# The value projection of an HGRN2 trunk in chunks of 512 features, token blocks apart, scaled out by ScalarE

## The reference

```python
def hgrn2_mixer(xn, w_in, lb, out_gain, w_out):
    proj = xn @ w_in                     # (256, 2048) @ (2048, 8192), float32
    q, fr, v, g = split(proj, 4)
    q = silu(q) * 128 ** -0.5
    f = lb + (1.0 - lb) * sigmoid(fr)
    k = 1.0 - f
    o = chunked_gated_recurrence(q, k, v, log(f))
    return (rms_norm(o, out_gain) * silu(g)) @ w_out
```

## Time and profile before

| | us |
|---|---|
| median of 3 runs (2339.4 to 2339.58) | 2339.45 |
| the profiled execution | 2340.2 |
| its span | 2338.4 |
| TensorE busy (share of the span) | 2328.3 (100%) |
| VectorE busy | 1691.0 (72%) |
| ScalarE busy | 1044.3 (45%) |
| granted TensorE clock | 0.999 |

### The profile page before, as it was taken

How to read it: one execution, slowest core, us unless ns; L and a number is a source line. 1 busy time by engine, 2 the same in 40 slices (tenths; PEclk the granted TensorE clock), 3 DMA queues, 4 the chain that set the end, 5 groups by cost and what they waited for, 6 DMA issues and landing times.

```text
span 2338.4 us, 37346 instructions
## 1 busy us (share of the span) xinstructions
PE 2328.3 (100%) x13212; PEld 2049.6 (88%) x13212; DVE 1691.0 (72%) x2147; ACT 1044.3 (45%) x1146; POOL 2.7 (0%) x8
## 2 busy tenths in 40 slices
PE   9999999999999999999999999999999999999998
PEld 8988888888888888888888888888888888888887
DVE  7978788768788788764545666666788788785444
ACT  7344443554444444434444444444444444443443
POOL 0000000000000000000000000000000000000000
PEclk9999999999999999999999999999999999999999
DMA  7555554565656656656565666565656656665664
GB/s 248 159 171 163 164 177 157 175 197 182 192 179 195 188 181 196 191 187 193 185 194 185 190 188 190 185 194 172 201 184 188 197 180 189 193 205 186 192 191 157
DMA packets 410284, 434.93 MB, mean 186 GB/s; under 512 B 13264, under 2 KB 386384, under 8 KB 410064
## 3 DMA queue, kind: packets, MB, share of 16 engines
q1 hardware_dynamic: 409616, 431.53, 59.1%
q10 hardware_dynamic: 576, 2.16, 0.3%
HBM read 431.54 MB, written 2.10 MB: 185 GB/s over the span
## 4 chain that ended last, share of the span: by engine, by line
PE 98%; DMA 1%; DVE 0%; ACT 0%; SPq 0%; issue 0%; DVEq 0%; ACTq 0%
PE acc L1071 54%; PE acc L1081 28%; PE acc L1117 3%; PE acc L1118 3%; PE acc L1116 3%; PE acc L1094 3%; PE acc L1103 1%; PE side L1233 1%; PE side L1212 0%; DMA h<-in_x 0%; DMA raw<-in_hgrn_w_in 0%; PE side L1228 0%; PE side L1063 0%; DVE w_parts L552 0%; PE side L1051 0%; ACT w_parts L333 0%
## 5 line engine op out<-in xcount | busy, mean ns | idle before, releaser
L552 DVE TENSOR_TENSOR w_parts<-raw,w_parts 128x1024 fp32r<-128x1024 f32 x816 | 979.9, 1222 | 578.9 <-PE acc L1081 417.6
L333 ACT ACTIVATE w_parts<-raw 128x1024 fp32r<-128x1024 f32 x816 | 856.4, 1058 | 990.8 <-PE acc L1071 764.0
L1071 PE MATMUL acc<-xn,w_parts 128*128 128x512 f32 x4352 | 1040.1, 391 | 1.4 <-ACT w_parts L333 1.0
L1071 PEld LDWEIGHTS acc<-xn,w_parts 128*128 128x128 f32 x4352 | 799.5, 188 | 156.4 <-issue 1.2
L1081 PEld LDWEIGHTS acc<-xn,w_parts 128*128 128x128 f32 x4352 | 557.5, 191 | 20.4
L1081 PE MATMUL acc<-xn,w_parts 128*128 128x256 f32 x4352 | 566.8, 283 | 0.0
L1071 PE MATMUL acc<-act,w_parts 128*128 128x512 f32 x1216 | 290.6, 391 | 0.0
L1071 PEld LDWEIGHTS acc<-act,w_parts 128*128 128x128 f32 x1216 | 223.5, 188 | 43.3
L1081 PEld LDWEIGHTS acc<-act,w_parts 128*128 128x128 f32 x1216 | 156.0, 191 | 6.0
L1081 PE MATMUL acc<-act,w_parts 128*128 128x256 f32 x1216 | 157.9, 283 | 0.0
L1116 PE MATMUL acc<-w_parts,act 128*128 128x512 f32 x352 | 137.3, 390 | 0.0
(11 more groups left out here) (124 smaller groups left out, 1020.7 us busy)
## 6 DMA issues: line engine op xcount, KB each, us to landing
raw<-in_ffn_w_up SPq DMA_DIRECT2D x352, 512.0 KB, 3.7
raw<-in_ffn_w_down SPq DMA_DIRECT2D x176, 512.0 KB, 4.3
raw<-in_hgrn_w_in SPq DMA_DIRECT2D x128, 512.0 KB, 3.8
raw<-in_sc_w_in SPq DMA_DIRECT2D x96, 512.0 KB, 4.6
raw<-in_hgrn_w_out SPq DMA_DIRECT2D x32, 512.0 KB, 3.9
raw<-in_sc_w_out SPq DMA_DIRECT2D x32, 512.0 KB, 4.2
h<-in_x SPq DMA_DIRECT2D x4, 512.0 KB, 7.8
final_w<-in_final_norm ACTq DMA_DIRECT2D x1, 1024.0 KB, 7.2
```

Of the source, the lines that this page charges most:

```text
L333: nc.scalar.activation(w_parts[:, c % RING, :, 0, :], raw[:, c % RING], ACT.Copy).then_inc(hi_ready, 1)
L552: v.tensor_tensor(w_parts[:, c % RING, :, 1, :], raw[:, c % RING], w_parts[:, c % RING, :, 0, :].bitcast(F32), ALU.subtract).then_inc(lo_r ...
L1071: o = mm(to[:, j, :], w[:, q, 0, j * P:(j + 1) * P], src[:, k * KW + q, :, :].rearrange("p n t -> p (n t)"), start=begin and q == 0, stop= ...
```

## The change

The value group alone is made in another way. Its chunks become 2 tiles of input features by 512 output features, 8 of them for the whole group, with no halves. A chunk has six matmuls of 512 columns a token block: four with the high part of the weights (tokens high and low, 2 tiles) and two with the low part. All six of a block add up in one bank, bank 0 of set 0 for block 0 and of set 1 for block 1. For a pair of chunks TensorE makes block 0 of both (highs, then lows), then block 1 of the first chunk (highs, lows, side work), then of the second. The wait for low parts is in block 0's lows; `hi_used` and `lo_used` count in block 1. Block 0's last matmul of the group counts `first_values_done`.

At the group's last chunk, behind the split of the chunk four ahead, ScalarE scales block 0 out of its bank into `vt`, then block 1, 512 columns each, and each gives a set back. VectorE has no part in it, `corr` isn't used, and the corrections of the phase are counted without the group's two.

```diff
-HGRN_IN = Phase(None, 4, 4, DT, scales=3)
+V_GROUP = 2
+HGRN_IN = Phase(None, 4, 4, DT, scales=3, wide_group=V_GROUP)
...
+            def values(i, c):
+
+                for b in range(T // P):
+                    if b == 0:
+                        act_e.wait_ge(first_values_done, at(i, 1, 1))
+                    else:
+                        act_e.wait_ge(lo_used, at(i, HGRN_IN.cpi, c + 1 + RING))
+                    nc.scalar.activation(vt[:, :, b, :], acc[:, b, 0, :].rearrange("p (j d) -> p j d", j=TG), ACT.Copy,
+                                         scale=rs[:, T + b:T + b + 1]).then_inc(acc_free, 1)
...
                             if not last:
                                 split(i, phase, c + RING)
-                            if ends and phase.corrections:
+                            if ends and g == phase.wide_group:
+                                values(i, c)
+                            elif ends and phase.corrections:
                                 correction(i, phase, g, part, c)
...
-                if phase is HGRN_IN and g == V_GROUP:
-                    for b in range(T // P):
-                        o = v.scalar_tensor_tensor(
-                            out=vt[:, part * TW:(part + 1) * TW, b, :],
...
+            def value_highs(c, b, src, k, begin):
...
+                for q in range(KC):
+                    for n in range(2):
+                        o = mm(acc[:, b, 0, :], x_block(src, k * KC + q, n, b), w[:, 2 * q:2 * q + 2, 0, :],
+                               start=begin and q == 0 and n == 0, stop=False)
+                return o
...
+            def value_run(i, first, src, chunks, between):
+
+                for b in range(T // P):
+                    for c, k, begin, end in chunks:
+                        if begin:
+                            pe.wait_ge(acc_free, at(i, HGRN_IN.api, V_GROUP * HGRN_IN.parts + b + 1))
+                        if b == 0:
+                            pe.wait_ge(hi_ready, at(i, HGRN_IN.cpi, c + 1))
+                        elif first:
+                            pe.wait_ge(mirror_ready, k * KC // TG + 1)
+                        high = value_highs(c, b, src, k, begin)
+                        if b:
+                            high.then_inc(hi_used, 1)
+                            value_lows(c, b, src, k, end).then_inc(lo_used, 1)
+                            between(c)
+                    if b == 0:
+                        for c, k, begin, end in chunks:
+                            pe.wait_ge(lo_ready, at(i, HGRN_IN.cpi, c + 1 + RING))
+                            low = value_lows(c, b, src, k, end)
+                            if end:
+                                low.then_inc(first_values_done, 1)
```

More of the change, by code:

```diff
@@ L58, with __init__ @@
 class Phase:
-    def __init__(self, before, n, groups, k_tiles, scales=0, corrects=True, parts=2):
+    def __init__(self, before, n, groups, k_tiles, scales=0, corrects=True, parts=2, wide_group=None):
         self.n, self.groups, self.cpg, self.parts = n, groups, k_tiles // KC, parts
         self.cpi, self.api = groups * self.cpg, groups * parts
-        self.scales, self.corrections = scales, self.api if corrects else 0
+        self.wide_group = wide_group
+        wide_parts = 0 if wide_group is None else parts
+        self.scales, self.corrections = scales, self.api - wide_parts if corrects else 0
         self.c0 = before.c0 + before.n * before.cpi if before else 0
@@ L69, in __init__, with wide @@
         assert self.cpi % RING == 0 and self.c0 % RING == 0 and self.api % SETS == 0
+    def wide(self, g):
+        return self.parts == 1 or g == self.wide_group
     def steps(self, first, g):
-        if self.parts == 1:
+        if self.wide(g):
             order = [(0, k) for k in range(self.cpg)]
@@ L80, in steps @@
             order = [(part, k) for part in range(2) for k in range(self.cpg // 2)]
-        last = self.cpg // self.parts - 1
+        last = self.cpg // (1 if self.wide(g) else self.parts) - 1
         return [(part, k, k == 0, k == last) for part, k in order]
@@ L262, in at, with rows_of, raw_slot @@
             return i * per + first
[L264 to L266 removed]
+        def rows_of(wide, w, k, part, col):
+            if wide:
                 return w[k * KC * P:(k + 1) * KC * P, bass.ds(col, GC)].rearrange("(k p) n -> p k n", p=P)
             return w[k * KW * P:(k + 1) * KW * P, bass.ds(col + part * GW, GW)].rearrange("(k p) n -> p k n", p=P)
[L270 to L272 removed]
+        def raw_slot(wide, c):
+            if wide:
                 return raw[:, c % RING].rearrange("p a n -> p (a n)").rearrange("p (k n) -> p k n", k=KC)
@@ L290, in body @@
                             sp.sem_inc(loads_begun, 1)
-                            sp.dma_start(raw_slot(phase, c), rows_of(phase, w, k, part, column(i, g))) \
+                            sp.dma_start(raw_slot(phase.wide(g), c), rows_of(phase.wide(g), w, k, part, column(i, g))) \
                                 .then_inc(w_loaded[c % RING], 16)
@@ L335, in correction @@
             def correction(i, phase, g, part, c):
-                done = hi_used if phase is HGRN_IN and g == V_GROUP else lo_used
-                act_e.wait_ge(done, at(i, phase.cpi, c + 1 + RING))
+                act_e.wait_ge(lo_used, at(i, phase.cpi, c + 1 + RING))
                 a = g * phase.parts + part
                 act_e.wait_ge(acc_free, at(i, phase.api, phase.a0 + a + SETS))
-                if phase is HGRN_IN and g == V_GROUP:
-                    for b in range(T // P):
[L344 to L348, removed]
+                nc.scalar.activation(corr[:], acc[:, a % SETS, :, T:], ACT.Copy).then_inc(corr_ready, 1)
+            def values(i, c):
[6 more added lines that the diff above has]
+                                         scale=rs[:, T + b:T + b + 1]).then_inc(acc_free, 1)
             def phase_of(phase, pieces, peel_last=False):
@@ L535, in body @@
                                 split(i, phase, c + RING)
-                            if ends and phase.corrections and not early:
+                            if ends and phase.corrections and not early and g != phase.wide_group:
                                 corrected(i, phase, g, part, into(g))
@@ L576, in corrected @@
                 a = g * phase.parts + part
-                dve.wait_ge(corr_ready, at(i, phase.corrections, phase.corr0 + a + 1))
-                if phase is HGRN_IN and g == V_GROUP:
-                    for b in range(T // P):
-                        o = v.scalar_tensor_tensor(
-                            out=vt[:, part * TW:(part + 1) * TW, b, :],
[L582 to L587, removed]
+                skipped = phase.parts if phase.wide_group is not None and g > phase.wide_group else 0
+                dve.wait_ge(corr_ready, at(i, phase.corrections, phase.corr0 + a - skipped + 1))
+                v.tensor_tensor(dst[:, part * TW:(part + 1) * TW, :], acc[:, a % SETS, :, 0:T], corr[:], ALU.add) \
+                    .then_inc(acc_free, 1)
             def await_corrected(i, phase, g):
@@ new lines, in value_highs, with value_lows @@
+                return o
+            def value_lows(c, b, src, k, end):
+                w = w_parts[:, c % RING]
+                for q in range(KC):
+                    o = mm(acc[:, b, 0, :], x_block(src, k * KC + q, 0, b), w[:, 2 * q:2 * q + 2, 1, :],
+                           start=False, stop=end and q == KC - 1)
+                return o
+            def value_run(i, first, src, chunks, between):
[18 more added lines that the diff above has]
+                                low.then_inc(first_values_done, 1)
@@ L1150, in body @@
                         for run in phase.runs(first, g, phase.cpg - RING * ends_here):
+                            if g == phase.wide_group:
+                                c0 = phase.c0 + g * phase.cpg
+                                value_run(i, first, src, [(c0 + kk, *steps[kk][1:]) for kk in run],
+                                          lambda c: between(i, first, g, c - c0))
+                                continue
                             chunks = []
@@ L1183, in body @@
                             for c, to, k, end in chunks:
[L1184 to L1188, removed]
+                                pe.wait_ge(lo_ready, at(i, phase.cpi, c + 1 + RING))
+                                feature_lows(to, c, src, k, end)
                             between(i, first, g, run[-1])
```

19 lines of the change are left out of this document (1 added, 18 removed).

## The result

| | before | after |
|---|---|---|
| median of 15 runs, us | 2339.58 (2339.31 to 2340.29) | 2344.14 (2343.89 to 2344.5) |
| profiled span, us | 2338.4 | 2342.4 |
| TensorE busy, us | 2328.3 | 2327.1 |
| granted TensorE clock | 0.999 | 0.999 |

The ratio is 1.0019, with a 95% interval from 1.0012 to 1.0027. The forecast was 2344.3 us. On which side of 0.2% it lies is another matter. The prediction drew its line at 0.2%, or 2344.13 us, and gave 0.59 to the slower side. Against the median of this comparison, 4.56 us is 0.195%, and the interval has the line in it.

What follows compares the result with a forecast made beforehand. TensorE, busy 2328.3 of 2338.4 us, was taken to bound the kernel. Per group, a gain of 0.37 and a loss of 1.59 us gave +1.22, over four groups +4.9: 2344.3 us from 2339.45, range 2343.2 to 2346.4.

Steps and rivals of the forecast that it cites:

- The place and the kind of the loss: At the output gate's opening, TensorE waits 1.48 us for ScalarE's copy of block 0; with the slow start, 1.59 us a group.
- S: Start of the last chunk's four high matmuls of block 1 in the value group; the wait's steps are counted from it.
- The hand-over to TensorE: From the end of ScalarE's copy to TensorE's start: 0.09 us, taken between VectorE's 0.05 and ScalarE's 0.14.
- The slow start behind it: After the wait, 16 wide matmuls start from an empty pipe: 3.93 us against 3.82, 0.11 us more a group.
- The gain: TensorE's own work in the value group falls from 26.78 to 26.41 us: 0.37 us a group, bounds 0.28 to 0.45.
- The wide matmuls behind a side stage: After the recurrence's small matmuls, wide ones lose 0.12 us over an unbroken row, at four stages a group.
- the long row: Wide matmuls into one bank, in the down projection's last block, start 0.2267 us apart; taken as the value group's pace.
- The sum: Gain and loss together: +1.22 us a group, +4.9 us over four groups, bounds 4.0 to 5.4.
- No wait: Rival: ScalarE hands over set 0 in time at the output gate's opening, leaving only the gain: 2338.0 us; chance 8%.
- Block 1 held by set 1: Rival: block 1's first matmul waits for VectorE's sum to empty set 1, about 0.5 us a group, 2346.3 us; chance 6%.
- The clock: Rival: TensorE's clock falls to 1.2 GHz in the four waits, 3.7 us a group, +15, 2359 us; chance 4%.
- The statement that ScalarE's and VectorE's other work costs nothing: Outside the new wait, changes to ScalarE's copies, VectorE's sums and low-part timing only gain slack; no size in time.

Runs made afterwards that it cites:

- The first experiment: The changed kernel with ScalarE's copy of block 0 ahead of the split of the chunk four ahead, not behind it; 2337.55 us, ratio 0.9991 to before.
- the second: The changed kernel with one more ScalarE copy of 512 columns, into an unread buffer, between the split and the copy of block 0; 2346.36 us, ratio 1.0030.
- the fifth experiment: The kernel with block 0's copy ahead of the split, with each low-weight matmul but a block's last made as two of 256 columns; 2340.1 us, ratio 1.0002.
- the third experiment: The changed kernel with three more chained ScalarE copies of 1024 columns between the split and the copy of block 0; 2364.32 us, ratio 1.0106.

## Why the prediction came out

**The place and the kind of the loss** were right: a wait of TensorE for ScalarE's copy at the opening of the output gate's group, in all four iterations, behind a split that itself waits for the last highs. The first experiment shows it by moving the copy, the second by lengthening the chain.

**The terms**, from the third iteration. The split started 1.21 us after S (1.20 forecast), the copy 0.96 later (0.96). The copy lasts 0.67 to 0.68 us (0.69 forecast). Less the 0.60 of a copy without a scale, that is 0.07 to 0.08 for the scale operand. The Trainium skill ("ScalarE: Activation LUTs", What ACT_TABLE_LOAD costs) gives 93 ns for it, a little more than was measured here. The hand-over to TensorE took 0.05 us (285.90 + 0.67, then 286.62), not 0.09: the 0.14 that I had averaged in came from the kernel's first matmul and was the wrong row for this; VectorE's 0.05 was the right one. Together the wait is 1.43 us where I had 1.48. The slow start behind it, 3.92 against 3.82 us for 16 matmuls, was 0.10 (0.11).

**The gain** was mis-sized most: 285.19 - 258.88 = 26.31 us against 26.78 in the earlier trace rows, 0.47 us a group and not 0.37. The pairs are as forecast (264.35 - 258.88 = 5.47). The wide matmuls behind a side stage start less slowly than I took them: four take 1.01 us (283.73 to 284.74), 0.10 over the long row's 0.907, where I had used the 0.12 that a full row of sixteen behind a stage loses; over four stages that is 0.08 of the 0.10 us. That this gain comes from having no narrow matmuls is shown by the fifth experiment.

**The sum** by these is 1.43 + 0.10 - 0.47 = 1.06 us for the third group. In the first iteration the wait cost a little more: TensorE's turn was at 81.42 and it started at 82.92, 1.50 us later. Over all four groups the two profiles give 4.35 us: TensorE came to the first value group at 55.12 us after and at 55.49 before, 0.37 earlier; and to the side stage behind the fourth one's wait at 392.24 against 388.26, 3.98 later. The profiled spans differ by 4.0 because of that earlier start, and such differences come without a change: the changed kernel and the third experiment's are the same up to the first group's last chunk, and their TensorE started it at 79.97 and at 79.68. The medians differ by 4.56, 0.2 more than the four groups account for, and no run shows where that comes from. I forecast 4.9: two errors of 0.05 and 0.10 us a group, both pointing the same way, put it about half a microsecond over the four groups of the profiles, and that it came within 0.3 us of the medians is in part luck. On whether the loss is over or under 0.2% the forecast leaned to the wrong side by a hair: a line that the forecast itself lay on can't be called, and 0.59 to 0.39 said little more.

**The rivals.** No wait: wrong, as the profile shows; its time (2338.0) is what the first experiment gives with the order changed (2337.55), since it was priced as the gain alone. Block 1 held by set 1: did not happen; block 1's first matmul ran at 261.63, 2.75 us after the group's start, with no wait on record. The clock: it did not fall behind the waits of 1.3 us, in none of four in the profile, and the 15 timed runs lie within 0.6 us, less than one fall. But I had it as a remote case, and it was near: at 1.9 us of idle it fell behind one wait of four. Its price was wrong too: I had 3.7 us for a fall, taking all 16 matmuls at 1.2 GHz, and a fall cost 1.4 to 1.6 in most cases and 2.8 once, as only a part of the 16 ran at half the clock.

The statement that ScalarE's and VectorE's other work costs nothing held: none of TensorE's waits past the start names anything but the copy.

## What to carry to other kernels

When a result moves to another engine or another place in an engine's order, find the instruction ahead of it and ask what that one waits for: here the copy's data were complete and the engine was idle, but a split in front of it waited for the very matmuls after which the bank was wanted. If a change makes a buffer live to the end of its group, its release belongs ahead of whatever waits for that end. On an engine that never waited, the gain in shape was small here (0.47 us a group), and one hand-over at the wrong place cost three times that (1.53 us).

## What the runs showed of the hardware

TensorE's clock fell behind short idle times in a kernel that is otherwise busy throughout. In the profiled executions the 16 wide matmuls behind a wait took 3.92 to 3.94 us at 2.4 GHz and 5.3 to 6.7 with a fall. There are four such waits in each: none had a fall at 1.3 us of idle, one at 1.9, one at 2.4, three at 2.9, all four at 4.5. Counted by steps of 1.6 us in the times of all runs, which is an inference, it was none of 60 waits at 1.3 us, two of 24 at 1.9 and ten of 16 at 2.9. Waits of one length came with a fall and without, so something beside the length decides, and no run here shows what. Nor does the fall have to come in the idle time: behind the first wait of 1.9 us the clock was full for over 1 us of work and fell then.

The Trainium skill ("TensorE: Matmul & The Clock Gate", HAM oscillation) warns of idle gaps, but of longer ones than the 1.9 us after which the clock fell here. Its section on psum-queue depth-cycling says that frequent micro-idles can do it too; here a single gap of 1.9 us did it once in four, and gaps of 1.3 us, four of them about 100 us apart, did not. A fall makes the same kernel's time take steps: 2346.2 or 2347.9 us with nothing changed.
